# Causal attention taken in periods of two items

## The reference

```python
p_s = masked_softmax(jnp.einsum('bqghd,bgqkd->bghqk', qr, k_sel), (kpos <= t[:, None])[:, :, None])
o_s = jnp.einsum('bghqk,bgqkd->bqghd', p_s, v_sel)
...
p_w = masked_softmax(jnp.einsum('bqghd,bkgd->bghqk', qr, kwin), m_w)
o_w = jnp.einsum('bghqk,bkgd->bqghd', p_w, vwin)
g = take(gates)
o = g[..., 0:1] * o_c + g[..., 1:2] * o_s + g[..., 2:3] * o_w
```

## The kernel before

| i mod 6 | query tile | branches | score columns for two heads | transposes |
|---|---|---|---|---|
| 0 | 0 | 2 | 512 | 4 |
| 1 | 1 | 2 | 1024 | 8 |
| 2, 3 | 2 | 1 | 768 | 6 |
| 4, 5 | 3 | 1 | 1024 | 8 |

## Time and profile before

### The profile page before, as it was taken

The page is one execution under the profiler, slowest core; times in us unless marked ns, Lnnn a source line. Parts: engine busy times, 40 slices in busy tenths (PEclk is TensorE's granted clock), DMA queues, the critical chain, the costliest instruction groups (busy, mean ns, idle before and its releaser), DMA issues.

```text
span 2016.0 us, 31718 instructions
## 1 busy us (share of the span) xinstructions
PE 1996.1 (99%) x12708; PEld 1670.8 (83%) x12708; DVE 1278.3 (63%) x2271; ACT 1055.6 (52%) x1754; POOL 722.5 (36%) x358
## 2 busy tenths in 40 slices
PE   8999999999999999999999999999999999999999
PEld 6778788989888887778889898878789987878997
DVE  6884566665647257873666655557777734777682
ACT  7752465444437327873644444556754444766441
POOL 3342134444444631003434444434024444412443
PEclk9999999999999999999999999999999999999999
DMA  4442133233332431002333332222013322211232
GB/s 162 126 141 73 48 98 105 96 104 105 105 97 92 144 98 31 12 2 98 105 105 97 103 105 95 94 95 84 12 63 105 106 95 93 84 32 53 96 105 93
DMA packets 62752, 179.28 MB, mean 89 GB/s; under 512 B 17792, under 2 KB 18176, under 8 KB 62608
## 3 DMA queue, kind: packets, MB, share of 16 engines
q1 hardware_dynamic: 47600, 168.04, 25.2%
q10 hardware_dynamic: 15008, 9.22, 1.7%
HBM read 171.97 MB, written 3.70 MB: 87 GB/s over the span
## 4 chain that ended last, share of the span: by engine, by line
PE 93%; DVE 3%; ACT 2%; issue 1%; POOL 0%; DMA 0%; ACTq 0%; DVEq 0%
PE banks L955 20%; PE banks L957 19%; PE banks L956 19%; PE banks L1073 6%; PE banks L1074 6%; PE banks L1075 6%; PE banks L1461 2%; PE banks L1482 2%; PE banks L1446 2%; PE banks L1571 1%; PE banks L1584 1%; PE banks L1556 1%; PE banks L1019 1%; PE banks L1562 1%; PE banks L1354 1%
## 5 line engine op out<-in xcount | busy, mean ns | idle before, releaser
L3457 POOL TENSOR_TENSOR w_lo<-raw,w_hi 128x1024 fp32r<-128x1024 f32 (+4 forms) x350 | 717.4, 2056 | 1277.4 <-ACT w_hi L1729 1122.3
L1729 ACT ACTIVATE w_hi<-raw 128x1024 fp32r<-128x1024 f32 (+2 forms) x274 | 263.8, 963 | 417.5 <-PE banks L957 292.2
L955 PE MATMUL banks<-a_lo,w_hi 128*128 128x512 f32 x832 | 329.1, 396 | 0.0
L955 PE MATMUL banks<-h_lo,w_hi 128*128 128x512 f32 (+1 forms) x800 | 321.2, 401 | 7.9 <-POOL w_lo L3457 7.9
L956 PE MATMUL banks<-a_hi,w_lo 128*128 128x512 f32 x832 | 324.4, 390 | 0.0
L957 PE MATMUL banks<-a_hi,w_hi 128*128 128x512 f32 x832 | 324.0, 389 | 0.0
L957 PE MATMUL banks<-h_hi,w_hi 128*128 128x512 f32 (+1 forms) x800 | 312.8, 391 | 0.0
L956 PE MATMUL banks<-h_hi,w_lo 128*128 128x512 f32 (+1 forms) x800 | 312.6, 391 | 0.0
L2597 DVE TENSOR_TENSOR x<-x,banks 128x512 f32<-128x512 f32 x168 | 115.2, 686 | 212.4 <-PE banks L957 212.4
L955 PEld LDWEIGHTS banks<-a_lo,w_hi 128*128 128x128 f32 x832 | 156.1, 188 | 39.2 <-DVE x L2597 7.4
L955 PEld LDWEIGHTS banks<-h_lo,w_hi 128*128 128x128 f32 (+1 forms) x800 | 149.8, 187 | 44.3 <-POOL w_lo L3457 7.9
(11 more groups left out here) (488 smaller groups left out, 4161.4 us busy)
## 6 DMA issues: line engine op xcount, KB each, us to landing
raw<-in_weights SPq DMA_DIRECT2D x311, 512.0 KB, 3.3
x<-in_x SPq DMA_DIRECT2D x4, 512.0 KB, 5.3
AT<-row_dram ACTq DMA_DIRECT2D x4, 512.0 KB, 8.4
out<-x SPq DMA_DIRECT2D x8, 256.0 KB, 2.0
eg<-row_dram ACTq DMA_DIRECT2D x8, 128.0 KB, 4.2
phase<-in_phase ACTq DMA_DIRECT2D x1, 706.0 KB, 4.1
phase<-in_phase ACTq DMA_DIRECT2D x1, 704.0 KB, 4.1
ld_dram<-Ld ACTq DMA_DIRECT2D x2, 256.0 KB, 3.6
```

The source lines that it names most:

```text
L955: mm(out, w_hi, x_lo, start=first, stop=False)
L1729: ins = f(c.w_hi[:, b % RING, cols], c.raw[:, b % RING, cols], ACT.Copy)
L3457: return nc.gpsimd.tensor_tensor(c.w_lo[:, slot, to], c.raw[:, slot, first:end], c.w_hi[:, slot, to].bitcast(F32), ALU.subtract)
```

## The change

TensorE's loop is replaced by three functions and a new order. In the period k it does s(2k), t(2k-3), v(2k-5), v(2k-4), t(2k-2), s(2k+1), so that two value blocks meet, and the last scores of a period meet the first of the next. On ScalarE exp(i) comes ahead of copy(i-2) where it came behind it, and a_hi one item later. On VectorE a_lo comes one item later. The instructions themselves are the same, and as many.

```diff
-    for i in range(len(NSA_ITEMS) + 3):
-        if i < len(NSA_ITEMS):
...
-        if 2 <= i < len(NSA_ITEMS) + 2:
...
-        if i >= 3:
...
+    def scores1(i):
...
+    def turned1(n):
+        j, qt, brs = NSA_ITEMS[n]
+        out = claim_pair(("t1", n))
+        for s in range(2):
+            for b in range(len(brs)):
+                pe.wait_ge(c.prob_ready, prob_count(n, s, b))
+                for kt in range(b * (qt + 1), (b + 1) * (qt + 1)):
+                    ins = nc.tensor.transpose(out[:, s, kt * P:kt * P + P], c.prob[:, n % 4, s, kt * P:kt * P + P], ident)
+        ins.then_inc(fill(("t1", n)), 1)
+
+    def values1(n):
...
+        read(("t1", n))
...
+    count1 = len(NSA_ITEMS)
+    for k in range(count1 // 2 + 1):
+        if 2 * k < count1:
+            scores1(2 * k)
+        if k > 1:
+            turned1(2 * k - 3)
+        if k > 2:
+            values1(2 * k - 5)
+        if k > 1:
+            values1(2 * k - 4)
+        if k:
+            turned1(2 * k - 2)
+        if 2 * k < count1:
+            scores1(2 * k + 1)
+    values1(count1 - 3)
+    turned1(count1 - 1)
+    values1(count1 - 2)
+    values1(count1 - 1)
```

ScalarE:

```diff
-    for i in range(len(NSA_ITEMS) + 3):
-        if 2 <= i < len(NSA_ITEMS) + 2:
-            key, (_, qt, brs) = ("t1", i - 2), NSA_ITEMS[i - 2]
-            n, end = i - 2, len(brs) * (qt + 1) * P
-            filled(key)
-            f(c.probT[:, n % 4, :, 0:end], c.pairs[bank[key][0] // 2][:, :, 0:end], ACT.Copy).then_inc(release(key), 1)
+    for i in range(len(NSA_ITEMS) + 4):
         if i < len(NSA_ITEMS):
             key, (_, qt, brs), end = ("s1", i), NSA_ITEMS[i], (NSA_ITEMS[i][1] + 1) * P
             act.wait_ge(c.nb_ready, i + 1)
...
             ins.then_inc(release(key), 1)
+        if 2 <= i < len(NSA_ITEMS) + 2:
+            key, (_, qt, brs) = ("t1", i - 2), NSA_ITEMS[i - 2]
+            n, end = i - 2, len(brs) * (qt + 1) * P
+            filled(key)
+            f(c.probT[:, n % 4, :, 0:end], c.pairs[bank[key][0] // 2][:, :, 0:end], ACT.Copy).then_inc(release(key), 1)
         if i in (5, 11):
             weights(first + 4 + i // 6)
-        if i >= 4 and (i - 4) % len(NSA_STEPS) == NSA_LAST:
-            j = (i - 4) // len(NSA_STEPS)
+        if i >= 5 and (i - 5) % len(NSA_STEPS) == NSA_LAST:
+            j = (i - 5) // len(NSA_STEPS)
```

VectorE:

```diff
-    for i in range(len(NSA_ITEMS) + 2):
+    for i in range(len(NSA_ITEMS) + 3):
...
-        if i >= 5 and (i - 5) % len(NSA_STEPS) == NSA_LAST:
-            out_parts((i - 5) // len(NSA_STEPS))
+        if i >= 6 and (i - 6) % len(NSA_STEPS) == NSA_LAST:
+            out_parts((i - 6) // len(NSA_STEPS))
```

More of the change, by code:

```diff
@@ new lines, in scores1 @@
+    def scores1(i):
+        j, qt, brs = NSA_ITEMS[i]
+        end, out, both = (qt + 1) * P, claim_pair(("s1", i)), slice(brs[0], brs[-1] + 1)
+        halves = [out[:, s, 0:len(brs) * end].rearrange("p (b k) -> p b k", b=len(brs)) for s in range(2)]
+        if i % len(NSA_STEPS) == 0 and j in NSA_PARTS_FROM:
+            pe.wait_ge(c.score_lo, NSA_PARTS_FROM[j])
+        for n, (q, k) in enumerate(((c.q_lo1, c.keys_hi), (c.q_hi1, c.keys_lo), (c.q_hi1, c.keys_hi))):
+            for s, r in enumerate(halves_of):
+                mm(halves[s], q[r, j, qt * P:end], k[r, both, j // 4, 0:end], start=n == 0, stop=False)
+        for part, first in ((0, 64), (1, 0)):
+            for s, r in enumerate(halves_of):
+                at = qt * P + 64 * part
+                ins = mm(halves[s][:, :, at:at + 64], c.causal16[r, first:first + P],
+                         c.causal16[r, 192:256].unsqueeze(1).to_broadcast([64, len(brs), 64]), start=False, stop=part == 1)
+        ins.then_inc(fill(("s1", i)), 1)
@@ new lines, in turned1 @@
+    def turned1(n):
[8 more added lines that the diff above has]
+    def values1(n):
+        j, qt, brs = NSA_ITEMS[n]
+        if n == 0:
@@ L1467, in program_tensor @@
                 read(("pcT", tt))
-        if i >= 3:
[L1469 to L1472, removed]
-                for s, o_rows in enumerate(halves_of):
[L1474 to L1485, removed]
+        if n % len(NSA_STEPS) == 0:
+            outs[j] = claim(("o1", j))
+            for s, o_rows in enumerate(halves_of):
+                r = slice(32 * ((2 * j + s) % 4), 32 * ((2 * j + s) % 4) + 32)
+                mm(outs[j][o_rows, :], c.vcb[r, 2 * (j // 4) + s, :], c.pcT[r, j // 2, :], start=True, stop=False)
@@ new lines, in values1 @@
+        read(("t1", n))
+        last = n % len(NSA_STEPS) == NSA_LAST
+        for b, br in enumerate(brs):
+            for kt in range(qt + 1):
+                for s, o_rows in enumerate(halves_of):
+                    v0, at = br * 256 + (2 * (j // 4) + s) * 64, (b * (qt + 1) + kt) * P
+                    ins = mm(outs[j][o_rows, qt * P:qt * P + P], c.v[:, kt, v0:v0 + 64], c.probT[:, n % 4, s, at:at + P],
+                             start=False, stop=last and kt == qt)
+        if last:
+            ins.then_inc(c.attn_out, 1)
```

## The result

The changed kernel takes 2025.1 us (median of 6 runs, 2024.3 to 2026.13) against 2018.54 us before: ratio 1.0028, 95% interval 1.0019 to 1.0038. It is slower, by 6.6 us where 10.3 were forecast. The profiled execution took 2024.75 us, with a span of 2022.9.

What follows compares the result with a forecast made beforehand. TensorE was taken to bound the attention, ScalarE at 82%. Steady rounds 8.6 us plus the end 1.7, beginning and clock nothing, made 10.3 us more: 2029.1 us from a median of 2018.83, range 2023 to 2034.

Steps and rivals of the forecast that it cites:

- TensorE's order: TensorE blocks of each period: two value blocks together save 0.15, scores behind scores 0.05; ready at 3.29, 4.39, 2.95 us.
- Period B: Period from the maximum of item 9: TensorE ready at 4.39 us, no wait for the copy, length 6.27 us.
- A: Period from the maximum of item 7: TensorE ready at 3.29, copy allows 4.38, so waits 1.09; length 5.89 us.
- the chain: Even items' transposes wait for maximum, exps, then the odd copy: 1.23 us more per six items, 8.6 in all.
- C: Period from the maximum of item 11: TensorE ready at 2.95, copy allows 3.69, so waits 0.74; length 5.85 us.
- to the exp 0.28: Lag from the end of VectorE's maximum, 797.94, to ScalarE's exp, 798.22: 0.28 us.
- The end: The last even item's transposes start 3.69 us after the last maximum in place of 2.02: 1.7 us more.
- The beginning: First items wait on exps in either order: counted at nothing, with 1 us either way in the range.
- the saved changes of kind decide: Rival: copies never late on TensorE, six items take 16.18 us, 4.2 us less in all, 2014.6 us; 5%.
- The chain without its lags: Rival: lags of 0.28 and 0.05 us before exp and transposes are hidden, 4.6 us less than forecast, 2024.5 us; 12%.
- VectorE was not late: Rival: maxima of all 21 periods start 0.3 us late, VectorE still scaling; 6 us more, 2035 us; 9%.
- no overhead goes: Rival: like kinds meeting on TensorE saves nothing; 1 us in all, 2030 us; 74% together with the forecast.

Runs made afterwards that it cites:

- the two halved copies: Changed kernel with half or less of the columns copied, for odd items in one run, even items in the other: 2020.13 us and 2023.86 us.
- the shifted period: Changed kernel with TensorE's period laid one item later, ScalarE and VectorE as in the changed kernel: 2021.15 us, ratio 1.0010.
- tensor_alone: Changed kernel with ScalarE's old order (copy ahead of exp), keeping TensorE's new order: 2054.43 us, ratio 1.0169.
- scalar_alone: TensorE's old order with ScalarE's new one (exp ahead of copy): 2043.21 us, ratio 1.0115.
- the second kernel with a better beginning: Period one item later from item 7 on, first 13 blocks reordered, ScalarE's first two copies ahead of exps 2 and 3: 2016.21 us, ratio 0.9982.
- the last two kernels: Period one item later with the first 13 blocks reordered, without and with ScalarE's first two copies moved earlier: 2015.69 us and 2016.21 us.
- odd_copies_half: Changed kernel, but copies of odd items move half of the columns or less: 2020.13 us, ratio 1.0008.
- copies_short: Changed kernel, but every copy moves 128 columns of each head only: 2017.32 us, ratio 0.9995.

## Why the prediction was right

*TensorE's order.* Right in the steady rounds. Between 799.45 and 801.79 the changed kernel has s11, s12 and t9 in 2.34 us; by the prediction's terms it is 0.97 - 0.12 + 0.07 + 0.63 + 0.80 = 2.35. Period B, which TensorE binds, came at 6.25 against 6.27. In the round shown above TensorE was ready for t12 at 3.79 after the maximum (806.16 to 808.27, and 1.68 for the two value blocks), where A has 3.29. The prediction put the weight conversions at nothing, as nothing would wait for the exps behind them. S14 does wait for one, and that cost no time only because the chain, at 4.16, was later still: here the nothing was right by luck.

*The chain.* Right as a mechanism: the waits stand at t(2k) in periods A and C and not in B, behind maximum, exp and copy, and the two halved copies show that it is these and no load.

*The size of its terms.* Here lies the error, 0.23 us in each of A and C: 5.66 and 5.63 against 5.89 and 5.85. The step "to the exp 0.28" was mis-sized. I read it as the lag between the end of the maximum at 797.94 and the exp at 798.22. But the earlier trace rows also hold the copy at 797.51, which ran for 0.81, to 798.32: ScalarE was busy with it, and the exp started as it ended. Where nothing else stands before, the after profile has 0.04 (801.75 to 801.79). Over seven rounds that is 7 x (18.01 - 17.54) = 3.3 us too much, B's 0.02 with it, and 0.2 at the end. The waits of the transposes, 8.0 us where 12 to 14 were forecast, are short by the same lag, and by what s14 took in two rounds.

*The end* was forecast at 1.7 and cost 1.4, less by the same lag. *The beginning*, counted at nothing with 1 us either way, gave back 0.8. Together: 10.3 - 3.3 - 0.2 - 0.8 = 6.0, the 5.9 measured in the attention. The medians differ by 0.7 us more, 6.6; that is inside the spread of the executions (2017.7 to 2021.2 us before), and no changed instruction explains it.

*The rivals.* That the saved changes of kind decide is refuted for this order; it is the time TensorE would have without the chain, and the shifted period comes near it. "The chain without its lags" was the nearest to what happened: one of its two lags was not there (0.04 us in place of 0.28), the other was (0.05). VectorE was not late in the changed kernel: it waits 27.8 us for scores in the steady part, and the maxima shown above, those of the chain, all follow such a wait. It was late in three of the experiments, for one round each, where a scaling met GpSimd's work. That no overhead goes is refuted by the merged value blocks (0.14 saved).

*The clock* was charged at nothing, rightly here: 1.00 over the stretch in the profile, with waits of up to 1.1 us. Several of the experiments show that this can't be taken for granted at the beginning.

## What to carry to other kernels

When an engine's list is reordered to save its own overhead, write down for every single buffer what must happen between one filling and the next, on which engines and in which order, and count the blocks that are left to cover it; here four blocks had to cover what six had covered. Items of different size make the phase of a period matter: the same order laid one item later turned a loss of 0.76 us a round into a gain of 0.65, but only with a beginning of its own. And a lag read between two rows is a lag only if the waiting engine was idle in it.

## What the hardware showed that was not expected

*TensorE's clock.* In four of the eleven profiles it fell to its lower level about 6 us after the first scores, behind pauses of which none was longer than 1.31 us. In the shifted kernel they were 0.83, 1.11 and 1.31 us. In tensor_alone, scalar_alone and the second kernel with a better beginning they were 0.83, 1.11 and 0.40, with the same blocks between them as in the kernel before, which in its profile has the same three pauses and kept the clock. So the blocks and pauses alone do not decide it; what else does is open. The kernel before shows both in its own executions: of the 21 beside the last two kernels, those with a mean clock of 1.000 took 2017.7 to 2018.8 us, those of 0.998 or less 2020.0 to 2021.7. The order still counts: all 11 executions of the shifted kernel have 0.998 or less, and with t0 ahead of s3 8 of 11 have 1.000.

*VectorE beside GpSimd.* In three profiles (odd_copies_half, copies_short, shifted) a scaling instruction of 128x512 that started within GpSimd's subtraction of 128x1024 took 2.60 to 2.61 us in place of 0.54, and ended 0.3 us after it. The maxima, which VectorE reads from PSUM, took their usual 1.22 us beside the same subtraction in the changed kernel (806.16, GpSimd 804.97 to 807.41). No run here moves that subtraction, so that it is the cause is read from the times only.
